# Later small transfers, a split first weight and identity matmuls in TensorE's pauses in a two-layer encoder trunk

## The chip, the cores and the metric

The kernel runs on one core of a Trainium2 chip. The metric is the device time of one execution in microseconds (us), the median over several runs. The profile is one further execution, recorded by the hardware profiler.

## What is computed

The reference runs two layers over 256 tokens of width 1024, in float32. Each layer is three sublayers, and each sublayer ends in a LayerNorm of the scaled residual plus the sublayer's output.

```python
for i in range(DEPTH):
    ...
    h = layer_norm(ALPHA * h + mix, ln_g[i, 0], ln_b[i, 0])
    h = layer_norm(ALPHA * h + memory_attention(h, mem, ...), ln_g[i, 1], ln_b[i, 1])
    if i % 2 == 0:
        ffn = swiglu(h, ffn_w_gate[j], ffn_w_up[j], ffn_w_down[j])
    else:
        ffn = moe_swiglu(h, moe_router[j], moe_w_gate[j], moe_w_up[j], moe_w_down[j])
    h = layer_norm(ALPHA * h + ffn, ln_g[i, 2], ln_b[i, 2])
```

Layer 0 mixes tokens with a sliding-window attention with sinks beside a stick-breaking attention, layer 1 with a forgetting attention. Layer 1 ends in a mixture of experts: a router (1024 to 8 columns) picks two of eight experts for each token, and each expert is a SwiGLU of width 3584.

## The kernel before

**Products.** All weights stream from device memory in chunks of 128 rows times up to four row tiles, 512 columns wide (1 MB; the first two chunks of all are half as large). SyncE issues the loads in order, with six buffers `raw`. A float32 product is made of three passes of a faster format: ScalarE copies a chunk to `w_hi` (line 1088), VectorE subtracts it from the original to get `w_lo` (lines 1456 and 1944), and TensorE multiplies high by high, high by low and low by high (lines 379 to 381). The semaphores `hi_made` and `lo_made` count the chunks that are split. The activations are split the same way: TensorE transposes 128x128 tiles of `X` into PSUM against the identity `ident` (line 423), ScalarE copies them to `xT_hi` (1088, called from `split_to`), VectorE makes `xT_lo` (1462). Four PSUM banks hold the eight tiles, two tiles each, so there are four copies of each kind, numbered 0 to 3 below. Chunk 0 of the first product needs copy 0 alone, chunk 1 copy 1, chunk 2 copies 2 and 3.

**Order.** The order of each engine's work is written out by hand, one function for each engine, and every engine runs its own list in that order. Waits are semaphores. A wait at the head of an engine's list holds back all that stands behind it on that engine, and nothing on the others.

**The start.** GpSimd writes the identity (lines 938 and 939), issues three small transfers (sinks of 4 KB, gate bias of 8 KB, `f_w` of 64 KB, lines 940 to 942) and builds masks, until it waits for `dist_abs` from VectorE (line 959). TensorE does 8 matmuls of the identity with itself (line 451; their output is overwritten), 16 transposes of `X` as its two halves land, 8 more identity matmuls (line 459), and then waits for the first chunk. ScalarE does the four `xT_hi` copies and then the splits; VectorE does two `xT_lo`, the first chunk's `w_lo`, and then the other two `xT_lo` (lines 1533 to 1536).

**The pauses.** At the end of the memory attention of each layer the function `normed_T` (lines 609 and 707) transposes the normalised `X`. The tokens are two blocks of 128, `t` = 0 and 1. VectorE normalises block 0 (`norm`, ending in line 1502), TensorE transposes its eight tiles, VectorE normalises block 1, and TensorE does the other eight. The other two LayerNorms of a layer put matmuls of the memory's key and value product around the transposes (`normed_T_beside`).

In layer 1 the router follows. `narrow` (lines 428 to 446) is a product of 24 small matmuls (lines 436 to 438), a copy of its result to `e_h` by VectorE (line 1440), and two small transposes (line 444). VectorE then finds the two experts of each token (lines 1814 to 1825), TensorE counts tokens by expert with five small matmuls (lines 746 to 753, "places"), VectorE makes the selection matrix `pick` (line 1835), and TensorE picks the first expert's rows with 16 matmuls in two halves (line 765, `pick_rows`). ScalarE and VectorE split the picked rows into `xe_hi` and `xe_lo`, half by half, and the experts' matmuls start.

Of the kernel before, what the change touches and what calls it, by code (L numbers as in the profile page):

```python
# [22 lines left out]
ALU = mybir.AluOpType  # L23
# [3 lines left out]
P = 128  # L27
# [4 lines left out]
def trunk(nc, x, mem, ln_g, ln_b, mem_wq, mem_wkv, mem_wo, ab_w_in, ab_sinks, ab_w_out,  # L32
# [76 lines left out]
    with ExitStack() as ctx:  # L109
# [144 lines left out]
        def sem(name):  # L254
            if name not in sems:
                sems[name] = ctx.enter_context(nc.semaphore(name))
            return sems[name]
# [101 lines left out]
        def _(pe):  # L359
# [52 lines left out]
            def transposes(key, src, tiles, b0, ready=None):  # L412


                dst = [claim(pe, f"{key}.{q // 2}", b0 + q // 2) for q in range(0, tiles, 2)]
                for t in range(TB):
                    for k in range(tiles):
                        if ready is not None and k % (tiles // 2) == 0:

                            name, n = ready[t]  # L420
                            pe.wait_ge(name, n if k else n - 1)
                        c = (k % 2) * SEQ + t * P
                        m = nc.tensor.transpose(dst[k // 2][:, c:c + P], src[:, t, k * P:(k + 1) * P],  # L423
                                                ident[:, :])
                        if t == TB - 1 and (k % 2 or k == tiles - 1):
                            m.then_inc(filled[b0 + k // 2], 1)

            def narrow(name, w_h, w_l, n, ready, staged, sb):
# [11 lines left out]
                m.then_inc(filled[4], 1)  # L440
                pe.wait_ge(sem(staged), 1)
# [5 lines left out]

            pe.wait_ge(sem("ident_made"), 1)

            for _ in range(8):  # L450
                nc.tensor.matmul(bank[7][:, 0:P], ident[:, :], ident[:, :], start=True, stop=True,
                                 skip_group_check=True)
# [5 lines left out]
            for _ in range(8):  # L458
                nc.tensor.matmul(bank[7][:, 0:P], ident[:, :], ident[:, :], start=True, stop=True,
                                 skip_group_check=True)  # L460
# [9 lines left out]
            for l in range(2):  # L470
# [138 lines left out]
                def normed_T(key, n):  # L609

                    transposes(key, X, KT, 4, ready=[(sem("normed"), NORMED * n + 2 * (t + 1)) for t in range(TB)])
# [95 lines left out]
                normed_T(f"{l}n1", 3 * l + 1)  # L707
# [34 lines left out]
            narrow("router", r_hi, r_lo, NE, ready, "r_T_made", e_h[0])  # L742
# [44 lines left out]

            pe.wait_ge(sem("picked"), 1)
# [134 lines left out]
        def _(pool):  # L923
# [8 lines left out]
            def link(ins):  # L932
# [7 lines left out]
            pool.dma_start(sinks[:, :], ab_sinks[0].partition_broadcast(P)).then_inc(sem("sink_in"), 16)  # L940
            pool.dma_start(gate_b[:, :], c_b_f[0].partition_broadcast(P)).then_inc(sem("b_in"), 16)
            pool.dma_start(f_w[:, :, :], c_w_in[0][:, 3 * D:3 * D + CH].rearrange("(k p) c -> p k c", p=P))\
                .then_inc(sem("f_in"), 16)
# [14 lines left out]

            pool.wait_ge(sem("dist_abs"), 1)
# [123 lines left out]
        def _(act):  # L1083
# [27 lines left out]
            def split_to(key, hi, tiles=range(4)):  # L1111

                for q in tiles:
                    b = wait_filled(act, f"{key}.{q}")
                    copy(hi[:, 2 * q:2 * q + 2, :].rearrange("p k t -> p (k t)"), b[:, :])\
                        .then_inc(sem("t_hi"), 1)
# [24 lines left out]
            split_to("0x", xT_hi)  # L1141
# [285 lines left out]
        def _(dve):  # L1427
# [114 lines left out]
            dve.wait_ge(sem("sink_in"), 16)  # L1542
            link(nc.vector.tensor_scalar(neg_sinks[:, :], sinks[:, :], -1.0, None, ALU.mult))

            for l in range(2):
# [59 lines left out]
                if l == 0:  # L1605
                    dve.wait_ge(sem("masks0"), 2)
                us = units(l)
# [427 lines left out]
```

## Time and profile before

| | |
|---|---|
| runs, us | 1654.07, 1654.28, 1656.89 |
| median, us | 1654.28 |
| the profiled execution, us | 1653.97 |
| its span from first to last instruction, us | 1652.0 |
| mean granted TensorE clock | 0.991 of full speed |
| TensorE matmul busy | 97% of the span |
| VectorE busy | 77% |
| ScalarE busy | 63% |
| GpSimd busy | 7% |

The page calls TensorE's matmuls PE and its weight loads PEld, VectorE DVE, ScalarE ACT, GpSimd POOL, SyncE SP. All positions in time are counted from the start of the span. The experts' part runs from about 678 us to the end; what comes before is the two layers' attention and layer 0's feed-forward part. The granted clock is given as a share of 2.4 GHz: 1.00 is 2.4 GHz and 0.50 is 1.2 GHz.

### The profile page before, as it was taken

Reading aid. Unit: us, or ns where it says so; the run is one execution under the profiler, and the core shown is the slowest. Engines: PE = TensorE matmul, PEld = TensorE weight load, DVE = VectorE, ACT = ScalarE, POOL = GpSimd, SP = SyncE. Lnnn points to the kernel's source line nnn. Section 1 sums busy time; section 2 is a strip of 40 time slices with the busy share of each in tenths; the row PEclk is TensorE's granted clock in tenths of the full one; section 3 lists DMA queues with packets and bytes.
Section 4 is the critical chain, followed back from the end, with each engine's and each line's share of the span. In section 5 each row is a group of like instructions: output and inputs, shape, how many; then the busy total and the mean of one; then the engine's idle time right before and its main releaser. Section 6 shows DMA issues by size and latency. Waiting matters only on the chain.

```text
span 1652.0 us, 21357 instructions
## 1 busy us (share of the span) xinstructions
PE 1605.9 (97%) x7602; PEld 1321.5 (80%) x7602; DVE 1269.3 (77%) x1188; ACT 1035.8 (63%) x935; POOL 118.3 (7%) x129
## 2 busy tenths in 40 slices
PE   8999999999999999999999999999999999999997
PEld 7777878888787687788888888888888888888775
DVE  5687565454746676789889889888888988988996
ACT  4464544443445543668777777777777777777673
POOL 2102010000113201000000000000000000000120
PEclk9999999999999999899999999999999999999999
DMA  9537655466455462899999999999999999999992
GB/s 334 177 103 234 225 171 186 130 224 208 154 193 177 143 221 72 290 373 362 389 378 376 388 366 386 389 362 388 389 359 383 388 369 385 388 358 390 361 362 99
DMA packets 238104, 480.11 MB, mean 291 GB/s; under 512 B 8224, under 2 KB 11328, under 8 KB 238048
## 3 DMA queue, kind: packets, MB, share of 16 engines
q1 hardware_dynamic: 229744, 454.06, 76.9%
q0 software_dynamic: 6288, 21.63, 4.1%
q10 hardware_dynamic: 2016, 3.67, 0.6%
q8 instruction: 35, 0.57, 0.2%
q14 instruction: 21, 0.17, 0.0%
HBM read 473.54 MB, written 11.03 MB: 293 GB/s over the span
## 4 chain that ended last, share of the span: by engine, by line
PE 84%; DVE 7%; issue 5%; DMA 3%; ACT 1%; POOL 1%; DVEq 0%; SPq 0%; POOLq 0%; ACTq 0%
PE bank L379 26%; PE bank L381 26%; PE bank L380 26%; DMA c_add<-gate_rows 2%; PE bank L845 1%; DVE w_lo L1944 1%; PE bank L423 1%; PE bank L666 1%; PE bank L644 1%; DVE w_lo L1456 1%; DVE X L1493 1%; DVE X L1502 1%; POOL c_add L926 1%; DMA raw<-in_ab_w_in_dram 0%; DVE stats L1482 0%
## 5 line engine op out<-in xcount | busy, mean ns | idle before, releaser
L1088 ACT ACTIVATE w_hi<-raw 128x2048 fp32r<-128x2048 f32 (+1 forms) x322 | 608.7, 1895 | 231.8 <-PE bank L381 222.5
L1944 DVE TENSOR_TENSOR w_lo<-raw,w_hi 128x2048 fp32r<-128x2048 f32 x221 | 503.1, 2290 | 81.8 <-ACT w_hi L1088 78.5
L1456 DVE TENSOR_TENSOR w_lo<-raw,w_hi 128x2048 fp32r<-128x2048 f32 (+1 forms) x96 | 211.2, 2205 | 135.3 <-ACT w_hi L1088 135.2
L379 PE MATMUL bank<-w_hi,xe_hi 128*128 128x512 f32 x736 | 293.0, 398 | 1.5 <-DVE w_lo L1944 1.5
L381 PE MATMUL bank<-w_hi,xe_lo 128*128 128x512 f32 x736 | 288.0, 391 | 0.0
L380 PE MATMUL bank<-w_lo,xe_hi 128*128 128x512 f32 x736 | 287.2, 390 | 0.0
L379 PE MATMUL bank<-w_hi,xT_hi 128*128 128x512 f32 (+1 forms) x560 | 218.1, 390 | 3.6 <-DVE w_lo L1456 3.4
L380 PE MATMUL bank<-w_lo,xT_hi 128*128 128x512 f32 (+1 forms) x560 | 214.1, 382 | 0.0
L381 PE MATMUL bank<-w_hi,xT_lo 128*128 128x512 f32 (+1 forms) x560 | 214.0, 382 | 0.0
L381 PEld LDWEIGHTS bank<-w_hi,xe_lo 128*128 128x128 f32 x736 | 138.4, 188 | 29.9
L379 PEld LDWEIGHTS bank<-w_hi,xe_hi 128*128 128x128 f32 x736 | 138.7, 188 | 29.1 <-DVE w_lo L1944 1.9
L380 PEld LDWEIGHTS bank<-w_lo,xe_hi 128*128 128x128 f32 x736 | 138.8, 189 | 27.4
L1944 DVE TENSOR_TENSOR w_lo_more<-raw,w_hi_more 128x2048 fp32r<-128x2048 f32 x63 | 144.2, 2289 | 18.4 <-ACT w_hi_more L1088 11.3
L1088 ACT ACTIVATE w_hi_more<-raw 128x2048 fp32r<-128x2048 f32 x64 | 122.8, 1919 | 28.1 <-PE bank L381 23.9
L379 PE MATMUL bank<-w_hi,eT_hi 128*128 128x512 f32 x320 | 125.8, 393 | 0.4 <-DVE w_lo L1944 0.4
L379 PEld LDWEIGHTS bank<-w_hi,xT_hi 128*128 128x128 f32 x560 | 105.9, 189 | 24.6 <-issue 5.0
L381 PE MATMUL bank<-w_hi,eT_lo 128*128 128x512 f32 x320 | 124.6, 389 | 0.0
L380 PE MATMUL bank<-w_lo,eT_hi 128*128 128x512 f32 x320 | 124.6, 389 | 0.0
L381 PEld LDWEIGHTS bank<-w_hi,xT_lo 128*128 128x128 f32 x560 | 106.0, 189 | 20.7
L380 PEld LDWEIGHTS bank<-w_lo,xT_hi 128*128 128x128 f32 x560 | 106.1, 189 | 19.4
L1944 DVE TENSOR_TENSOR w_lo<-raw_more,w_hi 128x2048 fp32r<-128x2048 f32 x40 | 91.4, 2286 | 3.7 <-ACT w_hi L1088 3.7
L1088 ACT ACTIVATE w_hi<-raw_more 128x2048 fp32r<-128x2048 f32 x40 | 76.6, 1916 | 25.2 <-PE bank L381 25.2
(281 smaller groups left out, 2150.8 us busy)
## 6 DMA issues: line engine op xcount, KB each, us to landing
raw<-in_moe_w_gate_dram SPq DMA_DIRECT2D x96, 1024.0 KB, 9.0
raw<-in_moe_w_up_dram SPq DMA_DIRECT2D x96, 1024.0 KB, 8.3
raw<-in_moe_w_down_dram SPq DMA_DIRECT2D x96, 1024.0 KB, 7.0
raw<-in_mem_wkv_dram SPq DMA_DIRECT2D x16, 1024.0 KB, 5.0
raw_more<-in_moe_w_up_dram SPq DMA_DIRECT2D x16, 1024.0 KB, 8.6
raw_more<-in_moe_w_gate_dram SPq DMA_DIRECT2D x16, 1024.0 KB, 8.6
raw_more<-in_moe_w_down_dram SPq DMA_DIRECT2D x16, 1024.0 KB, 7.4
raw<-in_c_w_in_dram SPq DMA_DIRECT2D x12, 1024.0 KB, 5.0
```

Of the source, the lines that this page charges most:

```text
L379: nc.tensor.matmul(d, xh, hi[:, k, :], start=(first and k == 0), stop=False)
L380: nc.tensor.matmul(d, xh, lo[:, k, :], start=False, stop=False)
L381: m = nc.tensor.matmul(d, xl, hi[:, k, :], start=False, stop=(last and k == n - 1))
L423: m = nc.tensor.transpose(dst[k // 2][:, c:c + P], src[:, t, k * P:(k + 1) * P], ident[:, :])
L644: m = nc.tensor.matmul(d[:, t * SEQ:(t + 1) * SEQ], QK[:, 2 * h + k, t * P:(t + 1) * P], MK[:, 2 * h + k, :], start=(k == 0), stop=(k == 1))
L666: m = nc.tensor.matmul(d[:, k * SEQ:(k + 1) * SEQ], MV[:, mb, c:c + P], PT_t[i % 2][:, mb * SEQ:(mb + 1) * SEQ], start=(mb == 0), stop=(mb ...
L845: m = nc.tensor.transpose(d[:, q * P:(q + 1) * P], e_h[j % 2][:, q * P:(q + 1) * P], ident[:, :])
L926: return nc.gpsimd.affine_select(out=dst, in_=dst, pattern=[[step, width]], compare_op=op, fill=fill, base=base, channel_multiplier=cm)
L1088: return nc.scalar.activation(dst, src, ACT.Copy)
L1456: tt(w_lo[s][:, 0:n], raw[c % NRAW][:, 0:n], w_hi[s][:, 0:n].bitcast(F32), ALU.subtract).then_inc(lo_made, 1)
L1493: link(nc.vector.scalar_tensor_tensor(out=xt, in0=xt, scalar=mean_var[:, t, 0:1], in1=gb[:, 0, :], op0=ALU.subtract, op1=ALU.mult))
L1944: tt(w_lo[s][:, :], raw_exp[r][:, :], w_hi[s][:, :].bitcast(F32), ALU.subtract).then_inc(lo_made, 1)
```

## The change

The three small transfers of GpSimd move behind its first masks, and behind a wait for the first three weight chunks to be split. VectorE's use of the sinks moves behind the layer 0 projections. ScalarE makes `w_hi` of the first chunk between copies 1 and 2 of `xT_hi`. The identity matmuls become a function, `keep_busy(bank, n)`, which issues `n` of them: at the start 16 and not 8 stand before the first product; 32 stand between the two blocks' transposes in `normed_T` of both layers' `n1`; and in the router 6 stand after its product, 14 after its transposes, and 8 after the places.

```diff
-            def transposes(key, src, tiles, b0, ready=None):
+            def transposes(key, src, tiles, b0, ready=None, busy=None):
                 dst = [claim(pe, f"{key}.{q // 2}", b0 + q // 2) for q in range(0, tiles, 2)]
                 for t in range(TB):
+                    if t and busy is not None:
+                        busy()
                     for k in range(tiles):
...
                 m.then_inc(filled[4], 1)
+                if busy is not None:
+                    keep_busy(busy, 6)
                 pe.wait_ge(sem(staged), 1)
...
+            def keep_busy(b, n):
+
+                for _ in range(n):
+                    nc.tensor.matmul(bank[b][:, 0:P], ident[:, :], ident[:, :], start=True, stop=True,
+                                     skip_group_check=True)
+
             pe.wait_ge(sem("ident_made"), 1)
-            for _ in range(8):
-                nc.tensor.matmul(bank[7][:, 0:P], ident[:, :], ident[:, :], start=True, stop=True,
-                                 skip_group_check=True)
+            keep_busy(7, 8)
...
-            for _ in range(8):
-                nc.tensor.matmul(bank[7][:, 0:P], ident[:, :], ident[:, :], start=True, stop=True,
-                                 skip_group_check=True)
+            keep_busy(7, 16)
...
-                normed_T(f"{l}n1", 3 * l + 1)
+                def mw0_bank(l=l):
+
+                    wait_emptied(pe, f"{l}mw0.0")
+                    return fillings[f"{l}mw0.0"][0]
+
+                normed_T(f"{l}n1", 3 * l + 1, busy=lambda: keep_busy(mw0_bank(), 32))
...
-            narrow("router", r_hi, r_lo, NE, ready, "r_T_made", e_h[0])
+            free = fillings["1mw0.0"][0]
+            narrow("router", r_hi, r_lo, NE, ready, "r_T_made", e_h[0], busy=free)
+            keep_busy(free, 14)
             pe.wait_ge(sem("taken_made"), 1)
...
+            keep_busy(free, 8)
             pe.wait_ge(sem("picked"), 1)
             pick_rows("xA")
...
-            pool.dma_start(sinks[:, :], ab_sinks[0].partition_broadcast(P)).then_inc(sem("sink_in"), 16)
-            pool.dma_start(gate_b[:, :], c_b_f[0].partition_broadcast(P)).then_inc(sem("b_in"), 16)
-            pool.dma_start(f_w[:, :, :], c_w_in[0][:, 3 * D:3 * D + CH].rearrange("(k p) c -> p k c", p=P))\
-                .then_inc(sem("f_in"), 16)
...
             nc.gpsimd.nop().then_inc(sem("masks0"), 1)
 
+            pool.wait_ge(lo_made, NSPL)
+            pool.dma_start(sinks[:, :], ab_sinks[0].partition_broadcast(P)).then_inc(sem("sink_in"), 16)
+            pool.dma_start(gate_b[:, :], c_b_f[0].partition_broadcast(P)).then_inc(sem("b_in"), 16)
+            pool.dma_start(f_w[:, :, :], c_w_in[0][:, 3 * D:3 * D + CH].rearrange("(k p) c -> p k c", p=P))\
+                .then_inc(sem("f_in"), 16)
             pool.wait_ge(sem("dist_abs"), 1)
...
-            split_to("0x", xT_hi)
+            split_to("0x", xT_hi, (0, 1))
+            split(0)
+            split_to("0x", xT_hi, (2, 3))
             split(NSPL - 1)
...
-            dve.wait_ge(sem("sink_in"), 16)
-            link(nc.vector.tensor_scalar(neg_sinks[:, :], sinks[:, :], -1.0, None, ALU.mult))
...
                 if l == 0:
                     dve.wait_ge(sem("masks0"), 2)
+                    dve.wait_ge(sem("sink_in"), 16)
+                    link(nc.vector.tensor_scalar(neg_sinks[:, :], sinks[:, :], -1.0, None, ALU.mult))
```

What stands on TensorE around `normed_T` of layer 0, before:

```order
L381 MATMUL bank<-w_hi_57,xT_lo 128x512
L423 MATMUL bank<-ident,X 128x128 x16
L379 MATMUL bank<-w_hi_55,xT_hi 128x512
L380 MATMUL bank<-w_lo_58,xT_hi 128x512
L381 MATMUL bank<-w_hi_55,xT_lo 128x512
```

and after the change:

```order
L425 MATMUL bank<-ident,X 128x128 x8
L455 MATMUL bank<-ident 128x128 x32
L425 MATMUL bank<-ident,X 128x128 x8
L379 MATMUL bank<-w_hi_55,xT_hi 128x512
L380 MATMUL bank<-w_lo_58,xT_hi 128x512
```

The 16 transposes are parted by 32 identity matmuls, and the feed-forward product stands directly behind. On TensorE from the end of the router's product to the first expert's rows, before:

```order
L438 MATMUL bank<-xT_lo,r_hi 8x256
L444 MATMUL bank<-ident,e_h_133 128x8 x2
L746 MATMUL bank<-taken,tri_lt 128x8
L748 MATMUL bank<-taken,ones 128x8
L750 MATMUL bank<-taken,tri_lt 128x8
L753 MATMUL bank<-taken,ones 128x8 x2
L765 MATMUL bank<-pick,X 128x128 x16
```

and after the change, with other line numbers for the same work:

```order
L440 MATMUL bank<-xT_lo,r_hi 8x256
L455 MATMUL bank<-ident 128x128 x6
L448 MATMUL bank<-ident,e_h_133 128x8 x2
L455 MATMUL bank<-ident 128x128 x14
L760 MATMUL bank<-taken,tri_lt 128x8
L762 MATMUL bank<-taken,ones 128x8
L764 MATMUL bank<-taken,tri_lt 128x8
L767 MATMUL bank<-taken,ones 128x8 x2
L455 MATMUL bank<-ident 128x128 x8
L779 MATMUL bank<-pick,X 128x128 x16
```

Three groups of identity matmuls now stand ahead of the transposes, the places and the picked rows. Nothing else moves on TensorE but the larger group at the start.

## Rows read from the trace of the kernel before

**Rows 1.** The page, its first part: busy time, share of the span, instructions.

```profile
PE 1605.9 (97%) x7602; PEld 1321.5 (80%) x7602; DVE 1269.3 (77%) x1188; ACT 1035.8 (63%) x935; POOL 118.3 (7%) x129
```

**Rows 2.** TensorE's waits: line, what it waited for, us in total, times, longest.

```profile
PE bank L423 <- DVE X L1502: 8.1, 3, 3.9
```

**Rows 3.** Timeline, first 13 us: start, duration, instructions, idle time before and releaser.

```profile
3.84 0.59 SPq L874 DMA_DIRECT2D mem_tok<-in_mem_dram  x1
...
6.70 2.06 ACT L1088 ACTIVATE xT_hi<-bank 128x512 fp32r<-128x512 f32 x4 [4.60 <-PE bank L423]
...
7.59 1.95 PE L459 MATMUL bank<-ident 128*128 128x128 f32 x16
9.94 1.06 ACT L1088 ACTIVATE w_hi<-raw 128x1024 fp32r<-128x1024 f32 x1 [1.17 <-DMA raw<-in_ab_w_in_dram]
11.02 1.23 DVE L1456 TENSOR_TENSOR w_lo<-raw,w_hi 128x1024 fp32r<-128x1024 f32 x1 [2.40 <-ACT w_hi L1088]
...
12.51 0.47 PE L379 MATMUL bank<-w_hi,xT_hi 128*128 128x512 f32 x1 [2.97 <-DVE w_lo L1456]
```

**Rows 4.** Groups of instructions, 7.5 to 9.6 us: busy us, mean ns of one, idle.

```profile
L459 PE MATMUL bank<-ident 128*128 128x128 f32 x16 | 1.9, 275 | 0.0
```

**Rows 5.** DMA queues from 6 to 10 us: packets, MB, share of 16 engines' time.

```profile
q0 software_dynamic: 83, 0.06, 24.0%
```

**Rows 6.** One stretch: busy time of each engine, then granted clock, DMA share, GB/s.

```profile
13.50:16.50 3.00, 3.00 (x8) 2.32 (x8) 1.08 (x1) 1.91 (x1) 0.00 (x0) 0.50 1.03 382
```

**Rows 7.** Timeline: TensorE's transposes of the memory, and its next wait.

```profile
19.70 1.91 PE L423 MATMUL bank<-ident,mem_tok 128*128 128x128 f32 x16
...
27.52 0.36 PE L379 MATMUL bank<-w_hi,xT_hi 128*128 128x256 f32 x1 [0.42 <-DVE w_lo L1456]
```

**Rows 8.** DMA issues, first 12 us: the memory tokens, size, us from issue to landing.

```profile
mem_tok<-in_mem_dram SPq DMA_DIRECT2D x1, 1024.0 KB, 13.3
```

**Rows 9.** Timeline of TensorE around `normed_T` of layer 0.

```profile
226.15 1.03 PE L423 MATMUL bank<-ident,X 128*128 128x128 f32 x8
231.11 1.78 PE L423 MATMUL bank<-ident,X 128*128 128x128 f32 x8 [3.93 <-DVE X L1502]
233.05 0.77 PE L379 MATMUL bank<-w_hi,xT_hi 128*128 128x512 f32 x1 [0.17 <-DVE xT_lo L1462]
```

**Rows 10.** The chain of waits there: start, duration, what.

```profile
233.82 0.43 PE bank L380
...
235.45 0.23 PE bank L381
```

**Rows 11.** Timeline in layer 1, from `normed_T` to the experts.

```profile
660.03 1.97 PE L423 MATMUL bank<-ident,X 128*128 128x128 f32 x8 [3.93 <-DVE X L1502]
...
661.38 2.48 DVE L1462 TENSOR_TENSOR xT_lo<-bank,xT_hi 128x512 fp32r<-128x512 f32 x4 [0.75 <-ACT xT_hi L1088]
...
662.22 0.37 PE L436 MATMUL bank<-xT_hi,r_hi 128*8 128x256 f32 x1 [0.23 <-DVE xT_lo L1462]
...
667.26 0.29 PE L444 MATMUL bank<-ident,e_h 8*128 8x8 f32 x2 [0.72 <-DVEq L1525]
...
669.32 0.59 PE L746 MATMUL bank<-taken,tri_lt 128*128 128x8 f32 x2 [1.77 <-DVE taken L1823]
...
672.49 5.28 PE L765 MATMUL bank<-pick,X 128*128 128x128 f32 x32 [0.87 <-DVE pick L1835]
...
676.02 0.60 ACT L1088 ACTIVATE xe_hi<-bank 128x512 fp32r<-128x512 f32 x1 [6.44 <-PE bank L765]
...
677.65 0.49 PE L379 MATMUL bank<-w_hi,xe_hi 128*128 128x512 f32 x1
```

**Rows 12.** Stretches of the same place, columns as in rows 6.

```profile
660.00:664.00 4.00, 3.74 (x17) 2.70 (x18) 3.12 (x5) 3.25 (x5) 1.58 (x3) 0.50 0.40 143
...
670.00:674.00 4.00, 3.13 (x15) 3.04 (x16) 2.04 (x9) 0.00 (x0) 0.00 (x0) 0.50 0.99 374
```

**Rows 13.** Same columns, in the last expert.

```profile
1544.00:1546.00 2.00, 2.00 (x6) 1.51 (x6) 2.00 (x1) 0.00 (x0) 0.00 (x0) 0.52 0.51 122
```

More of the change, by code:

```diff
@@ L426, in transposes, with narrow @@
                             m.then_inc(filled[b0 + k // 2], 1)
-            def narrow(name, w_h, w_l, n, ready, staged, sb):
+            def narrow(name, w_h, w_l, n, ready, staged, sb, busy=None):
                 dst = claim(pe, f"{name}0", 4)
@@ L607, in _, with normed_T @@
                 pair[0] = kv_pair + (1 if l == 0 else 2)
-                def normed_T(key, n):
-                    transposes(key, X, KT, 4, ready=[(sem("normed"), NORMED * n + 2 * (t + 1)) for t in range(TB)])
+                def normed_T(key, n, busy=None):
+                    transposes(key, X, KT, 4, ready=[(sem("normed"), NORMED * n + 2 * (t + 1)) for t in range(TB)],
+                               busy=busy)
                 def normed_T_beside(key, n, name):
```

## The prediction

> **What bounds the kernel now.** I read the page's busy shares first. TensorE is busy in 97% of the span [rows 1], so a change tells only where it starts TensorE's work earlier or later, lengthens it, or changes its clock. Then its waits [rows 2]: the longest group is on VectorE's normalisation, 8.1 us in three waits, up to 3.9 us each. The timelines show where. At the start TensorE ends its identity matmuls at 9.54 and starts the first product at 12.51, behind ScalarE's `w_hi`, which began at 9.94 as soon as the chunk had landed, and VectorE's `w_lo` [rows 3]. In each layer's `normed_T` it stands still for 3.93 us [rows 9, 11]. Behind the second follow pauses of 0.72, 1.77 and 0.87 us [rows 11]. After each pause the granted clock is at 0.50, that is 1.2 GHz, for a while: 13.50 to 16.50 [rows 6], from about 231.8 to 235.3 (matmul steps of 0.43, then 0.23 us) [rows 10], and in 660 to 664 and 670 to 674 [rows 12]. So the change is about four stalls and the slow stretches behind them.
>
> **The price of an identity matmul.** Eight of them are 16 records of 275 ns each, which overlap: together 1.95 us at full clock [rows 3, 4]. The spacing is (1.95 - 0.275) / 15 = 0.112 us a record, 0.223 us a matmul. At half clock the eight transposes of layer 1 give (1.97 - 0.47) / 7 = 0.21 a record (0.47 is an estimate of a slow record's own length, from slow steps of 0.43 [rows 10]), 0.43 a matmul. So at full clock 32 take 7.1 us, 16 take 3.6, 14 take 3.1, 8 take 1.8 and 6 take 1.3. TensorE's list is in order: what exceeds a pause delays what stands behind.
>
> **The start.** GpSimd's queue took 24.0% of the 16 DMA engines between 6 and 10 us, that is 0.96 us [rows 5]. Without it in front, the first chunk lands between 0.96 us earlier and no earlier; a row nearer than this there isn't, and I take 0.9: 9.0. `xT_hi` copies 0 and 1 end at 6.70 + 2.06 / 2 = 7.7 [rows 3], so ScalarE is free, and would be with all four (8.8). Its new order costs nothing: copies 2 and 3 end by 11.2, VectorE wants them behind `w_lo`, and TensorE only in chunk 2. `w_hi` runs 9.0 to 10.1, `w_lo` 10.2 to 11.4, and the first product starts at 11.6, 0.9 earlier. The 16 identity matmuls end at 7.59 + 3.6 = 11.2, just before: they cost nothing, but bar a gain above 1.3. With TensorE busy up to 0.4 us before, I take the clock to stay at 1.00. Before, the 24 matmuls of chunks 0 and 1 took 19.70 - 12.51 = 7.2 us [rows 3, 7]; at steps of 0.23 they take 5.5. That is 1.7 more. The memory's transposes then start at 17.1; their data were issued at 3.84 [rows 3] and landed 13.3 us later [rows 8], at 17.1, and land about 0.9 earlier now, so they don't wait. The next wait, 0.42 us at 27.52 [rows 7], hangs on these transposes by `mT_hi`, `w_hi` and `w_lo`, moves with them and stays. The later small transfers take the same 0.96 us of the DMA engines at about 18 to 28. There they meet chunks that TensorE needs 5.5 us apart, and the first chunks they meet are not waited for. GpSimd, which now stands at its new wait until about 17.5, has behind it in its list the masks that wait for VectorE until about 22 in any case; its three issues fit in between. VectorE's step on the sinks moves behind the projections, some 40 us later than the transfer lands. All this is nothing; without that slack it would be at most the 0.96 us again. **Start: -2.6 us**, between -1.7 (no earlier landing, clock kept) and -3.0.
>
> **Layer 0's pause.** The first eight transposes end at 231.11 - 3.93 = 227.18, their issue at 227.05. 32 identity matmuls last to 227.05 + 7.1 = 234.2, and only then come the other eight, at 231.11 before: 3.1 late [rows 9]. `X` is long ready, and the path from them to the product (1.94 us before) is about 0.1 shorter at full clock: the product starts at 236.0, 3.0 late. What the clock gives back is the slow stretch from 233.05 to 235.45: a first step of 0.77 and four of 0.35 to 0.43 in place of 0.47 and 0.23 [rows 3, 9, 10], together 1.0. All of TensorE's work behind follows without a pause, so nothing hides the rest. **Layer 0: +2.0 us**, between -1.1 (the pause exactly filled) and +3.0 (no clock gained).
>
> **Layer 1's pauses.** Step by step at full clock [rows 11]. The second transposes start 3.1 late, at 663.1. The router's product started 2.19 after them and did so on the first `xT_lo`; 0.1 shorter, it starts at 665.1. Its 24 matmuls at 0.113 take 2.7 (4.3 before; VectorE's four `xT_lo` need 2.48, and are not the limit), end 667.8 against 666.54: 1.3 late. Then 6 identity matmuls last 1.3, while the copy to `e_h` needed 0.72: the two transposes start at 669.1, 1.9 late. VectorE's search needed 2.06 from there to the places; 14 identity matmuls behind 0.2 us of transposes last 3.1: the places start at 672.4, 3.1 late. Their ten records take 1.2 and not 2.3 (669.32 to 672.49 less the 0.87 of idle time; the clock was at 0.50 [rows 12]): `pick` is ready 2.0 late, at 674.5. But 8 identity matmuls after the places (673.5) last to 675.3, so picking starts 2.8 late. Its 32 records take 3.6 and not 5.28: it ends at 678.9, as does the split of the first half (half the records 1.8, then the 1.63 us from 676.02 to 677.65). The experts start at 678.9 against 677.7. SyncE's load of the experts' seventh chunk waits for the router's product and is 1.3 late, like its use: nothing. **Layer 1: +1.2 us.** Between -4.4 (every pause exactly filled: product 1.7, places 1.0, picking 1.7 faster) and +12 (the clock lost, below).
>
> **The sum** is -2.6 + 2.0 + 1.2 = +0.6 us. The profiled execution's own time is 1653.97 with a span of 1652.0; 0.6 more is 1654.6. It is 0.3 below the median of the runs, so against the median it would be 1654.9; I take 1654.6. All other work keeps its place: the experts' part is a chain of matmuls that starts 0.6 later.
>
> **Rivals.** (1) **The fillers fit.** If an identity matmul took half of what I read, all five groups would end inside their pauses: -2.6 - 1.1 - 4.4 = -8.1 us, 1645.9. The Trainium skill ("TensorE: Matmul & The Clock Gate", Back-to-back issue gap) gives about 56 ns between 128-column matmuls at the full clock; by it the 64 records of 32 matmuls would take 3.6 us, less than the pause of 3.93. Against it stand the 16 records of rows 3 and 4 in this kernel, with the same operands, at twice that spacing. 8%. (2) **Slower: the clock falls in the router all the same.** Between the last transposes (664.0) and the router's product (665.1) a gap of 1 us stays. Before, 0.29 us of work between pauses of 0.72 and 1.77 was too little to keep the clock [rows 11, 12]. If it falls once in there, the identity matmuls at 0.43 last 2.6, 6.0 and 3.4 us, over 1.3, 3.1 and 1.8: 5.8 more, and the 1.6, 1.1 and 1.7 that I booked for a faster product, places and picking are gone too. Layer 1 is then +1.2 + 5.8 + 4.4 = +11.4, the whole +10.8: 1664.8. It decides from the clock at 665 on. 9%. (3) **A smaller start.** The chunk lands no earlier since other bytes take the room: -1.7, the sum +1.5, 1655.5. 15%, within 0.2%. (4) **More gained than booked,** by a first chunk that lands earlier than 9.0, overruns partly taken up by VectorE's waits, or the slow stretch in the last expert [rows 13], which cost about 1.7 us while TensorE was busy and need not come again: 1650 to 1652. 14%, half of it beyond 0.2%. (5) Both overruns a little longer, with a new wait for a chunk behind them since ScalarE's and VectorE's splits begin 3 us later: 1658. 6%, half of it beyond.
>
> **How the numbers follow.** My forecast, 1652.5 to 1656.5, has 48%. 0.2% is 3.3 us, about what a measurement here can tell from no change: 1651.0 to 1657.6 is "same". Faster: 8 + 7 = 15%. Slower: 9 + 3 = 12%. Same: 48 + 15 + 7 + 3 = 73%. The range of 8 in 10 reaches from case 4 to case 5: 1650.0 to 1658.0; cases 1 and 2 are outside.
>
> **What would show it.** The record of 32 identity matmuls should be 64 long and 7.1 us, in both layers, with transposes directly behind and no idle time there. The first product should start near 11.6 with the clock at 1.00 to 17. The small transfers should be issued near 17.5. The router's product should start near 663.1 + 2.0 less the 0.6 gained up to there (2.6 - 2.0), and the clock be 1.00 from 655 to 680. It would be wrong if identity matmuls ran at another spacing in a stretch of 64, or if the clock fell with TensorE busy.

## The result and the profile after

The changed kernel took 1657.82 us (median of 12 runs, 1654.79 to 1659.58). The kernel before, run beside it, took 1653.82 us (12 runs, 1650.48 to 1656.89). The ratio is 1.0021, with a 95% interval of 1.0014 to 1.0029: about 3.5 us slower (4.0 between the two medians), just above the 0.2% that I had set as the bound of "same". The profiled execution of the changed kernel took 1659.53 us with a span of 1657.6 and a granted clock of 0.994. That is 5.6 us more than the span of before, 1652.0.

The first line of the page, against [rows 1]:

```profile
PE 1623.4 (98%) x7802; PEld 1340.4 (81%) x7802; DVE 1269.2 (77%) x1188; ACT 1036.2 (63%) x935; POOL 120.2 (7%) x129
```

There are 200 more matmul records, and TensorE is busy for 17.5 us more. The group of stalls of [rows 2] has gone, and the kernel is none the faster for it. The timeline of the first 17 us, against [rows 3, 7]:

```profile
7.42 3.74 PE L455 MATMUL bank<-ident 128*128 128x128 f32 x32
7.80 1.06 ACT L1104 ACTIVATE w_hi<-raw 128x1024 fp32r<-128x1024 f32 x1 [0.37 <-DMA raw<-in_ab_w_in_dram]
...
8.89 1.22 DVE L1474 TENSOR_TENSOR w_lo<-raw,w_hi 128x1024 fp32r<-128x1024 f32 x1 [0.62 <-ACT w_hi L1104]
...
10.91 0.48 PE L379 MATMUL bank<-w_hi,xT_hi 128*128 128x512 f32 x1
...
16.41 0.72 POOL L971 DMA_DIRECT2D sinks<-in_ab_sinks_dram  x1 [11.48 <-DVE w_lo L1474]
16.47 1.91 PE L425 MATMUL bank<-ident,mem_tok 128*128 128x128 f32 x16
```

`w_hi` begins 2.14 us earlier and the first product 1.60 us earlier. `w_lo` ends at 10.11, but TensorE is at its identity matmuls until about 10.9. The memory's transposes come 3.23 us earlier. What the small transfers took from the weight stream shows in the DMA queues from 6 to 10 us (packets, MB, share of the 16 engines' time), before and after:

```profile
q1 hardware_dynamic: 484, 0.94, 69.6%
q0 software_dynamic: 83, 0.06, 24.0%
```

```profile
q1 hardware_dynamic: 812, 1.60, 104.5%
```

Queue q1 is the weight stream, q0 is GpSimd's (the profile's shares can come out a little above 100%). With 0.06 MB of q0 beside it, the stream moved 0.66 MB less.

The timeline in layer 0, against [rows 9]:

```profile
224.18 1.03 PE L425 MATMUL bank<-ident,X 128*128 128x128 f32 x8
...
225.05 7.31 PE L455 MATMUL bank<-ident 128*128 128x128 f32 x64
...
228.33 1.41 DVE L1520 SCALAR_TENSOR_TENSOR X<-X,rstd,gb 128x512 f32<-128x512 f32 x2
...
232.20 1.04 PE L425 MATMUL bank<-ident,X 128*128 128x128 f32 x8
...
234.08 0.47 PE L379 MATMUL bank<-w_hi,xT_hi 128*128 128x512 f32 x1 [0.85 <-DVE xT_lo L1480]
```

VectorE has `X` ready at 229.74, and TensorE takes it up at 232.20. In between it works at nothing that anyone needs. The same place in layer 1, up to the experts, against [rows 11]:

```profile
659.04 1.03 PE L425 MATMUL bank<-ident,X 128*128 128x128 f32 x8
...
659.91 7.31 PE L455 MATMUL bank<-ident 128*128 128x128 f32 x64
...
667.06 1.04 PE L425 MATMUL bank<-ident,X 128*128 128x128 f32 x8
...
668.94 0.28 PE L438 MATMUL bank<-xT_hi,r_hi 128*8 128x256 f32 x1 [0.85 <-DVE xT_lo L1480]
...
671.68 1.50 PE L455 MATMUL bank<-ident 128*128 128x128 f32 x12
...
673.11 0.29 PE L448 MATMUL bank<-ident,e_h 8*128 8x8 f32 x2
...
673.33 3.39 PE L455 MATMUL bank<-ident 128*128 128x128 f32 x28
...
676.56 0.29 PE L760 MATMUL bank<-taken,tri_lt 128*128 128x8 f32 x2
...
679.46 3.74 PE L779 MATMUL bank<-pick,X 128*128 128x128 f32 x32
683.17 0.49 PE L379 MATMUL bank<-w_hi,xe_hi 128*128 128x512 f32 x1
```

The clock, against [rows 12]: stretches of after (length, PE, PEld, DVE, ACT and POOL busy, then the granted clock, DMA share and GB/s). The last row lies in layer 1's `normed_T`, the first three in the two mixers, where the profile of before has 1.00:

```profile
78.00:80.00 2.00, 2.00 (x11) 1.34 (x8) 1.44 (x9) 2.00 (x4) 0.00 (x0) 0.50 0.03 11
428.00:430.00 2.00, 1.10 (x3) 0.92 (x4) 2.00 (x4) 2.00 (x3) 0.00 (x0) 0.76 0.04 7
556.00:558.00 2.00, 1.37 (x8) 0.86 (x8) 2.00 (x3) 1.40 (x6) 0.00 (x0) 0.50 0.00 0
662.00:664.00 2.00, 2.00 (x20) 2.00 (x20) 1.86 (x6) 0.00 (x0) 0.00 (x0) 1.00 0.03 8
```

So the clock held where identity matmuls stand, and fell at three places where the diff changes nothing.

**Where the time is.** I cut every profile at the same six instructions of TensorE: one behind the first scores of layer 0's mixer (near 78), a weight wait near 159, the transposes of layer 0's `n2` (near 426), a weight wait near 588, the `e_h` wait of the last expert (near 1528) and a `y` wait near 1638. Each number is the distance in us from one cut to the next; the kernels are described below.

```
kernel             to 78   78-159  159-426  426-588  588-1528  1528-1638
                                   (pause             (router)
                                    layer 0)
before             78.59   80.82   266.61   162.25   939.61    110.57
before again  e5   76.82   81.79   267.47   163.98   938.14    110.17
after              75.28   82.15   268.60   166.26   941.13    110.62
after again   e1   76.06   80.78   268.60   163.06   941.12    110.22
start only    e2   75.35   80.84   266.48   162.27   939.43    110.10
pauses only   e3   77.69   80.75   268.57   164.57   941.25    110.65
layer 0 only  e6   78.58   80.76   268.59   162.64   940.23    110.21
layer 1 only  e7   77.89   82.16   267.47   163.90   941.03    111.12
transfers     e8   75.09   82.06   267.30   163.90   938.37    110.17
fit           e4   75.60   80.84   265.65   164.25   935.80    110.40
fit, no router e12 75.95   80.76   265.63   163.02   938.31    110.65
```

The stretches that the diff doesn't touch go with the granted clock. From 78 to 159 us the profiles with a fall near 80 (e5, after, e7, e8) take 81.79 to 82.16, and those without 80.75 to 80.84. From 426 to 588 before and e2 have no fall and take 162.25 and 162.27; e1, e6 and e12, with some 3.4 us at half clock, take 162.64 to 163.06; e5, e7, e8 and e4, with about 7 us, take 163.90 to 164.25; after, with some 10 us in two places, takes 166.26. Only e3 is long (164.57) without a fall.

In the profile the changed places sum to -3.3 (start) + 2.0 (layer 0) + 1.5 (layer 1) = +0.2 us. The other +5.4 lie in 78 to 159 (+1.3) and 426 to 588 (+4.0), in code that the diff doesn't touch. The experiments ask whether the change brings these on.

### The profile page after: what moved, and what is told of

Its sections match the earlier page's. It is cut to its first block, busy times and chain, and to the rows that moved or that the text cites. A ratio compares the mean times of both kernels' runs of the same rounds, so it can differ in the third digit from the quotient of the medians.

```text
span 1657.6 us, 21757 instructions
## 1 busy us (share of the span) xinstructions
PE 1623.4 (98%) x7802; PEld 1340.4 (81%) x7802; DVE 1269.2 (77%) x1188; ACT 1036.2 (63%) x935; POOL 120.2 (7%) x129
## 3 DMA queue, kind: packets, MB, share of 16 engines
HBM read 473.54 MB, written 11.03 MB: 292 GB/s over the span
## 4 chain that ended last, share of the span: by engine, by line
PE 84%; DVE 6%; issue 5%; DMA 2%; ACT 1%; POOL 1%; DVEq 0%; ACTq 0%; POOLq 0%
PE bank L379 25%; PE bank L381 25%; PE bank L380 25%; DVE w_lo L1962 2%; PE bank L455 2%; DMA c_add<-gate_rows 2%; PE bank L860 1%; PE bank L425 1%; PE bank L673 1%; PE bank L651 1%; DVE w_lo L1474 1%; POOL c_add L941 1%; DMA y_got<-y_rows,row_i 0%; DVE X L1511 0%; PE bank L545 0%
## 5 line engine op out<-in xcount | busy, mean ns | idle before, releaser
L1104 ACT ACTIVATE w_hi_more<-raw 128x2048 fp32r<-128x2048 f32 x64 | 122.9, 1920 | 28.0 <-PE bank L381 23.8
```

The source lines that it names most:

```text
L1104: return nc.scalar.activation(dst, src, ACT.Copy)
```

## The experiments

The runs of one chip share the runs of the kernel before: e1 to e4 (before 1654.6), e5 to e8 (1654.3), e9 to e12 (1654.17). Each median is of 11 or 12 executions, but of 5 in e3 and e4. "By the ratio" means the measured ratio times the time of before; it differs from the distance of the medians by up to 0.9 us.

### e1: the changed kernel again

No edit.

> The changed kernel once more, for a second profile and more times beside the others. In its first profile the granted clock fell to 0.50 at about 78, 429.5 and 556 us, in the attention parts, which the change does not touch; the kernel before had no such stretch there and one at 1543. Theory A (the places of these stretches differ from run to run and are chance): in this profile they lie elsewhere or are fewer, the offset to the kernel before is -3.3 us from the start, +2.0 from layer 0's pause and +1.5 from layer 1's, and the median lies 0 to 2 us above the kernel before. Theory B (the change brings them on, since TensorE comes to the attention parts without a slow stretch before): they come again at the same places, and the median lies 3 to 5 us above.

Measured: 1656.58 us (11 runs), ratio 1.0011 (1.0002 to 1.0020), 2.0 us over before; span of the profile 1653.4. The stretches 78 to 159 and 426 to 588 are back at 80.78 and 163.06, near those of before, while the two pauses stand where they stood (268.60 and 941.12). The start takes 76.06, 0.8 more than in the first profile. So most of the +5.4 belonged to that execution, and not to the kernel.

### e2: the start alone

```diff
-                normed_T(f"{l}n1", 3 * l + 1, busy=lambda: keep_busy(mw0_bank(), 32))
+                normed_T(f"{l}n1", 3 * l + 1)
...
-            narrow("router", r_hi, r_lo, NE, ready, "r_T_made", e_h[0], busy=free)
-            keep_busy(free, 14)
+            narrow("router", r_hi, r_lo, NE, ready, "r_T_made", e_h[0])
...
-            keep_busy(free, 8)
```

> The kernel before with the start's part of the change alone: later small transfers, ScalarE's new order, 16 identity matmuls. My theory: the first product at 10.9 us as in the changed kernel, the offset to the kernel before -3.3 us until layer 0's pause, and all of it kept: median 1650.5, 3.3 us faster. Rival (slow stretches in the attention parts come with the early start): the clock falls near 78 us in the profile and the median gains only 1 to 2 us.

Measured: 1652.17 us, ratio 0.9990 (0.9981 to 0.9999); span 1648.0, 4.0 under that of before, of which the start has 3.24. In the medians 2.4 us are gained (1.7 by the ratio), less than my 3.3, though the clock does not fall near 78 us as the rival had it.

### e3: the pauses alone

The start is that of before (small transfers early, ScalarE's old order, 8 identity matmuls); the 32, 6, 14 and 8 stay.

```diff
-            keep_busy(7, 16)
+            keep_busy(7, 8)
...
-            split_to("0x", xT_hi, (0, 1))
-            split(0)
-            split_to("0x", xT_hi, (2, 3))
+            split_to("0x", xT_hi)
```

> The kernel before with the identity matmuls in the pauses alone (32, 32, 6, 14, 8), the start as before. My theory: +2.0 us in layer 0 and +1.5 in layer 1, median 3.5 us above the kernel before. Rival (the fillers also bring on slow stretches in layer 1's attention): 5 to 7 us above, with the clock at 0.50 near 430 or 555 us.

Measured: 1659.95 us, ratio 1.0035 (1.0021 to 1.0049), 5.3 us slower: the rival's 5 to 7, but without its falls of the clock. In place the two pauses cost 1.96 and 1.64 against the profile of before. Another 2.3 lie in 426 to 588, where the clock of this execution did not fall. GpSimd waited longer there for its transfers of the gates. Its waits from 520 to 556 us (what it waited for, then total, times, longest), before and then e3:

```profile
POOL c_add L926 <- DMA c_add<-gate_rows: 14.8, 6, 3.2
```

```profile
POOL c_add L941 <- DMA c_add<-gate_rows: 17.1, 6, 4.1
```

This is 2.3 us more for six transfers of the same size, in the same place. The changed kernel's profile has 17.0 there. From its first mask on `c_add` behind 513 us to its last before 555, GpSimd took 37.4 us in before, 39.7 in e3 and 38.9 in after. In the whole stretch TensorE waited 2.2 us for VectorE's `P` in e3 and 0.6 in before. That the late gates cause these waits is likely, since VectorE adds `c_add` to the scores that `P` is made from; no run alters the gates alone.

### e4: the same groups, sized to the pauses

At 0.223 us each, 17 take 3.8 us, 3 take 0.7, 7 take 1.6 and 4 take 0.9.

```diff
-                    keep_busy(busy, 6)
+                    keep_busy(busy, 3)
...
-                normed_T(f"{l}n1", 3 * l + 1, busy=lambda: keep_busy(mw0_bank(), 32))
+                normed_T(f"{l}n1", 3 * l + 1, busy=lambda: keep_busy(mw0_bank(), 17))
...
-            keep_busy(free, 14)
+            keep_busy(free, 7)
...
-            keep_busy(free, 8)
+            keep_busy(free, 4)
```

> The changed kernel with the groups in the pauses cut to what the pauses hold: 17, 17, 3, 7 and 4 identity matmuls at 0.223 us. My theory (the loss in the pauses is the overrun, and shorter groups keep the clock as well): layer 0's pause costs -1.1 us instead of +2.0, layer 1's -4 instead of +1.5; median 8 us below the changed kernel and 5 to 8 below the kernel before. Rival (the shorter groups leave enough idle time for the clock to fall): the clock is at 0.50 behind a pause and the gain over the kernel before is 3 us or less.

Measured: **1647.62 us** (1646.45 to 1648.23, 5 runs), ratio 0.9954 (0.9941 to 0.9968), 7.0 us faster than before. This version beats both kernels. Its timeline, layer 0 and then the router:

```profile
228.17 1.32 PE L425 MATMUL bank<-ident,X 128*128 128x128 f32 x8
...
230.11 0.47 PE L379 MATMUL bank<-w_hi,xT_hi 128*128 128x512 f32 x1 [0.62 <-DVE xT_lo L1480]
...
660.06 0.28 PE L438 MATMUL bank<-xT_hi,r_hi 128*8 128x256 f32 x1 [0.62 <-DVE xT_lo L1480]
...
662.80 0.83 PE L455 MATMUL bank<-ident 128*128 128x128 f32 x6
...
663.68 0.29 PE L448 MATMUL bank<-ident,e_h 8*128 8x8 f32 x2
...
663.90 1.83 PE L455 MATMUL bank<-ident 128*128 128x128 f32 x14
...
665.74 0.39 PE L760 MATMUL bank<-taken,tri_lt 128*128 128x8 f32 x2
...
667.89 3.84 PE L779 MATMUL bank<-pick,X 128*128 128x128 f32 x32
```

The 32 picking records take 3.84 us, and not the 5.28 of [rows 11]. Layer 0's stretch is 0.96 under that of before, the router's 3.81 under; against the means below over the profiles without groups it is 1.4 and 3.4. The mechanism of the change is sound; its numbers are about twice too large.

### e5: the kernel before again

No edit. The question was whether the falls in the mixers come without the change.

> The kernel before once more, for a second profile of it. Open after the first five profiles: layer 1's mixer, from the wait near 426 to the one near 588 us, took 162.25 and 162.27 us in the two kernels without identity matmuls in the pauses and 163.1, 164.3, 164.6 and 166.3 us in the four with them. Theory A (chance: it is clock falls and GpSimd's waits for its gate transfers, which come in some executions of any kernel): this profile has 162 to 166 too, and as likely over 163 as not. Theory B (the groups bring it on): 162.3 again.

Measured: 1653.91 us, ratio 0.9998 (0.9988 to 1.0009). Its stretches of 80 to 82 and 556 to 558, columns as above:

```profile
80.00:82.00 2.00, 2.00 (x5) 1.61 (x6) 1.93 (x11) 1.65 (x2) 0.73 (x1) 0.50 0.00 0
556.00:558.00 2.00, 2.00 (x11) 2.00 (x10) 1.74 (x7) 0.12 (x1) 0.00 (x0) 0.50 0.46 108
```

The kernel before has both falls itself in this execution, with 81.79 and 163.98 in the two stretches. The theory that the change brings them on has fallen.

### e6 and e7: the pauses of one layer alone

Both have the start of before. e6 fills layer 0's pause only:

```diff
-                normed_T(f"{l}n1", 3 * l + 1, busy=lambda: keep_busy(mw0_bank(), 32))
+                normed_T(f"{l}n1", 3 * l + 1, busy=(lambda: keep_busy(mw0_bank(), 32)) if l == 0 else None)
```

> The kernel before with the 32 identity matmuls in layer 0's pause alone. My theory: from the wait near 159 to the one near 426 us 268.6 us instead of 266.6, so +2.0, and the rest as in the kernel before: median 1.5 to 2.5 us above it. Theory B of the run before (the group brings on a longer mixer in layer 1): 163 to 166 us from 426 to 588 and a median 3.5 to 5 above.

e7 fills those of layer 1 (`if l == 1`, and the 6, 14 and 8).

> The kernel before with the identity matmuls in layer 1's pause and in the router alone (32, 6, 14, 8). My theory: from the wait near 588 us to the one in the last expert near 1528 941.1 us instead of 939.6, so +1.5, median 1 to 2 us above the kernel before. Layer 1's mixer stands before these groups in TensorE's list, so by theory B it takes 162.3 us; by theory A anything from 162 to 166.

Measured: e6 1658.55 us, ratio 1.0022 (1.0010 to 1.0033); e7 1657.51, ratio 1.0014 (1.0005 to 1.0023). By ratio that is 3.6 and 2.3 us over before, and both are above what I expected. In place e6 has +2.0 in its pause and e7 +1.4 in its own, as predicted. The profile of e6 has a span 2.5 over that of before, so the median's other microsecond or more isn't in the execution that was profiled.

The table shows one more thing. With the groups of the change a stretch is always the same (268.57 to 268.62, and 941.00 to 941.25, with e9 below). Without any it varies: 266.48 to 267.47 (five profiles, mean 267.07) and 938.14 to 940.23 (five, mean 939.16), since the clock behind a pause is down for longer in one execution than in the next. Around layer 0's pause it is below 1.00 from 230 to 236 us in the first profile of before, with 0.95, 0.50 and 0.69 in its three stretches of 2 us, and from 228 to 236 in e5, with 0.77, 0.50, 0.50 and 0.53. Against the means the groups cost 1.5 and 2.0 us.

The start varies in the same way. To the first cut, the five profiles with the old start (before, e5, e3, e6, e7) take 76.82 to 78.59, mean 77.91; the five with the whole new one (after, e1, e2, e4, e12) take 75.28 to 76.06, mean 75.65. That is -2.3 and not -3.3.

### e8: only the small transfers moved

Of the change, only GpSimd's three transfers, and VectorE's use of the sinks, are moved. 8 identity matmuls and ScalarE's order are as before.

> The kernel before with the later small transfers alone (ScalarE's order and 8 identity matmuls as before). If the early landing is what the start gains by, the first chunk's w_hi can begin only at about 8.5 us, behind all four xT_hi copies, instead of 7.8; the first product starts near 11.6 and TensorE stands idle from about 9.4 to then. My theory: the clock still falls behind that idle time as in the kernel before, so the start gains 0.9 to 1.3 us instead of 3.3. Rival (2.2 us of idle time are too few for a fall): 2.6 us.

Measured: 1651.50 us, ratio 0.9982 (0.9974 to 0.9991), 3.0 us faster by the ratio and 2.8 by the medians. That is the rival's gain and not mine. Its first product:

```profile
8.16 1.06 ACT L1102 ACTIVATE w_hi<-raw 128x1024 fp32r<-128x1024 f32 x1
...
10.74 0.47 PE L379 MATMUL bank<-w_hi,xT_hi 128*128 128x512 f32 x1 [1.76 <-DVE w_lo L1470]
```

```profile
11.00:13.00 2.00, 2.00 (x10) 1.62 (x10) 1.80 (x3) 0.85 (x1) 0.00 (x0) 1.00 1.03 421
```

The first product is 0.17 us earlier than in the profile of the whole change. The clock holds behind an idle time of 1.76 us, where it fell behind 2.97 [rows 3, 6] (it fell behind 2.57 in e3, and held behind 2.49 in e5). So all that the start gains here comes from the transfers. ScalarE's order and the 8 more identity matmuls bring nothing here. The 16 even hold the product back: in all five profiles of the whole new start it stands directly behind them, 0.55 to 1.16 us after `w_lo` ended (0.80 in after, 0.94 in e1, 1.16 in e12), where it follows 0.26 us behind in e8. They begin only when the transposes of `X` are done, at 7.42 in after and at 8.19 in e1. This run is faster than e2 in the medians too, by 0.7 us on another chip, which is less than I would call shown.

### e9: the changed kernel with the mixers' pauses covered

Groups of 5, 3, 2, 9 and 6 identity matmuls stand in addition where the clock fell, near 78, 555 and 428 us.

```diff
                     d = claim(pe, f"{l}t{i}", b)
+                    keep_busy(b, {(0, 1): 5, (1, 13): 3, (1, 14): 2}.get((l, i), 0))
+                    pe.wait_ge(sem(f"p_ready{l}"), i + 1)
...
+                    if (l, p) == (1, 6):
+                        keep_busy(7, 9)
...
+                    if key == "0n2":
+                        wait_emptied(pe, "0dn1.0")
+                        keep_busy(fillings["0dn1.0"][0], 6)
```

> The changed kernel with more identity matmuls, sized to the waits, where the profiles show chance falls of the clock: 5 in layer 0's mixer (before the second head's transposes, a wait of 1.27 us), 6 behind layer 0's last normalisation (1.55 us), and 3, 9 and 2 at the end of layer 1's mixer (0.74, 2.28, 0.61 us). What the runs so far leave open: by its parts in the profiles (-3.3 start, +1.5 to +2.0 layer 0, +1.5 to +2.0 layer 1) the changed kernel should be level with the kernel before, its median is 2 to 4 us above. Theory (chance falls in the mixers make up the rest and the spread): no fall at 78, 430 and 555 us in the profile, median 2 to 3 us below the changed kernel's 1656.6 to 1657.8, so 1654 to 1655, spread under 2 us. Rival (the rest is elsewhere): median above 1656.

Measured: 1656.22 us, ratio 1.0013 (1.0004 to 1.0022). The three falls are gone from its profile, and the kernel is still 2 us over before, as the rival had it. The profile shows the clock down in the last expert, near 1544, where before and e1 have it too, and near 1588, where neither does:

```profile
1544.00:1546.00 2.00, 2.00 (x6) 1.52 (x6) 2.00 (x2) 0.00 (x0) 0.00 (x0) 0.50 0.68 255
1588.00:1590.00 2.00, 2.00 (x7) 1.54 (x6) 2.00 (x3) 0.00 (x0) 1.89 (x1) 0.50 0.92 224
```

Its last stretch (1528 to 1638) is 112.24 against 110.57 of before. I had expected 1654 to 1655; the rest over before isn't in those three falls.

### e10 and e11: the sized groups with the mixers covered

e10 is e4 with the additions of e9. e11 has 12 at the start in place of 16.

> The kernel with groups cut to the pauses (17, 17, 3, 7, 4) with the same additions in the mixers. Theory: 1 to 3 us below the 1647.6 of the cut groups alone, so 1645 to 1647, with falls only in the last expert and at the end. Rival: no lower than 1647.6.

> The same with 12 identity matmuls in front of the first product in place of 16. In the changed kernel the first product started at 10.91 us, 0.8 behind the first w_lo, held by the 16; with later transfers alone and 8 it started at 10.74. Theory: the first product at 10.3, 0.5 us earlier than with 16, median 0.3 to 0.6 lower. Rival: with less cover the clock falls behind the start, 1 us slower.

Measured: e10 1649.69 us, ratio 0.9974 (0.9963 to 0.9984); e11 1649.10, ratio 0.9970 (0.9961 to 0.9980). Both gain some 4 to 5 us over before, and neither is better than e4 (7.0, on another chip). In e10's profile the clock falls near 126, and near 1580 behind a wait for VectorE that is 1.45 us long in before:

```profile
1579.53 0.80 PE L379 MATMUL bank<-w_hi,xe_hi 128*128 128x512 f32 x1 [3.49 <-DVE w_lo L1968]
```

Covering the mixers is not worth its lines. Whether 12 at the start would do better than 16 stays open: the first chunk happened to be split later in e11's profile, whose first product is at 11.03 behind an idle time of 0.97.

### e12: the sized groups without the router's

```diff
-            narrow("router", r_hi, r_lo, NE, ready, "r_T_made", e_h[0], busy=free)
-            keep_busy(free, 7)
+            narrow("router", r_hi, r_lo, NE, ready, "r_T_made", e_h[0])
...
-            keep_busy(free, 4)
```

> The changed kernel with 17 identity matmuls in each normed_T and none in the router. It tells what the router's groups bring once they fit. Theory (the clock falls behind the router's pauses of 0.7 and 1.8 us whether or not the one before is covered): a slow stretch near 670 us, the router's part 938 us or more from the wait near 588 to the one near 1525 in place of 935.8, median 2 to 3 us above the cut groups' 1647.6. Rival (17 in normed_T are enough to carry the clock over the router's pauses): level with it.

Measured: 1649.76 us, ratio 0.9973 (0.9964 to 0.9982). The clock is down in the router's picking again:

```profile
666.89 6.79 PE L778 MATMUL bank<-pick,X 128*128 128x128 f32 x32 [0.87 <-DVE pick L1851]
```

```profile
668.00:670.00 2.00, 2.00 (x11) 2.00 (x11) 1.73 (x1) 0.00 (x0) 0.00 (x0) 0.50 1.05 408
```

The router's stretch is 938.31 against e4's 935.80. The 3, 7 and 4 together bring 2.5 us there, and 2.1 in the medians. The medians are less certain: e4 ran on another chip with 5 executions, and e10, which has the router's groups and the covered mixers and ran beside e12, is level with it.

## Why the prediction was right, and where it was not

The measured time lies inside the range (1650.0 to 1658.0), near its upper end. The forecast of +0.6 us was too low: by the ratio it measured +3.5, and +1.8 in the second comparison. By my own bound of 0.2% the first is just "slower" and the second "same". That the time lies inside the range is in part luck. The upper end stood for rival (5), longer overruns and a new wait for a chunk. The overruns were as forecast, and layer 0's stretch, with +1.99 for +2.0, leaves no room for such a wait; what took the time up there was something else, told below.

**The price of an identity matmul was right.** 64 records take 7.31 us in both layers, for 7.1 predicted; the spacing of 0.112 us read from 16 records holds for 64. Rival (1), that the groups fit, was wrong for the changed kernel. e4 shows what such a fit gives: 1647.6, where I had put 1645.9. Against the profile of before layer 0 then gains 0.96 (for 1.1) and layer 1 gains 3.8 (for 4.4). By the means it is 1.4, 3.4 and 2.3 at the start, 7.1 in all, where the medians show 7.0. Of the two prices that the prediction weighed, the 56 ns that the Trainium skill ("TensorE: Matmul & The Clock Gate", Back-to-back issue gap) gives for an isolated matmul of 128 columns and the 112 ns of the row, the row was the one to follow. The same section gives about 81 ns for a stream in which each matmul has its weight load, as here; by that the 64 records would take 5.2 us, an estimate, and not fit the pause either.

**Layer 0 was right:** +2.0 predicted, +1.99 in the profile. Counted from the first transposes, the second begin 8.02 us later, against 4.96 before: 3.06 late. The product behind them is 3.0 late (9.90 against 6.90), and 1.0 comes back by the clock.

**Layer 1 was right within 0.3 us,** at each step. Counted from the first transposes (655.07 before, 659.04 after), the places start at 17.5 (predicted 17.3), the picking at 20.4 (20.2) and the experts at 24.1 (23.8; before 22.6). Each is late by what the group in front exceeds its pause. Of the losses here, the last group's is the plainest: `pick` is ready at 678.55, and TensorE starts on it at 679.46.

**Rival (2) did not come about.** The clock stays at 1.00 through the router. It did not fall behind the 0.85 us of idle time that remain before its product (668.94). Nor did rival (3): the first chunk landed earlier. Of rival (4) the early landing came about and the time did not.

**The start was mis-sized against the profile:** -3.3, for -2.6 predicted and -3.0 as the end of its range. The term that failed is the landing of the first chunk. I had priced the small transfers by their share of the DMA engines, 0.96 us, and put the landing at 9.0. It was at 7.80, 2.1 us earlier than before. One execution overstates it, though. With the old start `w_hi` began between 9.07 and 9.94 in five profiles, mean 9.60, and with the whole new one between 7.80 and 8.43, mean 8.15: 1.5 us earlier, for the 0.9 in my sum. The engines' share understates what such transfers cost the stream beside them: from 6 to 10 us the stream moved 0.87 to 1.01 MB in those five and 1.44 to 1.61 MB in the other five and e8. The second term is the clock's part. It was 1.7 predicted and measured 1.63 (the memory's transposes 5.56 us behind the first product, for 7.19), but in e5 the clock of the kernel before doesn't fall at the start, behind 2.49 us of idle time, and there was nothing to give back. By the means of five profiles the start is worth 2.3. The later small transfers and ScalarE's order, priced at nothing, cost nothing that a profile shows. I was right that the 16 identity matmuls could bar a gain above 1.3 (they held it at 1.6), but gave them no price. The third term is theirs: they hold the product back by 0.3 to 0.9 us, and the clock keeps without the 8 more in e8.

**The last expert's slow stretch costs nothing.** In rival (4) I put 1.7 us on it [rows 13]. The stretch from 1528 to 1638 takes 110.10 to 110.57 with it (before, e1, e2, e5, e6, e8, e4) and no less without it (110.62 in after, 110.65 in e3, 111.12 in e7). VectorE's `w_lo` is the later one there: TensorE's wait for it near 1585 is 1.45 us in before and 1.13 in e1, and 2.06 in after and 2.10 in e3, where no slow stretch precedes it.

**The sum failed in what it left out.** I wrote that all other work keeps its place. In the profiled executions the changed stretches sum to +0.2. But the code between them takes a different time from execution to execution, by 1.4 us (80.75 to 82.16) from 78 to 159 and by 4.0 us (162.25 to 166.26) from 426 to 588; the two profiles of the kernel before are 1.0 and 1.7 apart there. One profile against another can therefore mislead by more than the effect in question. This explains the profile's +5.6: falls of the clock near 80, 430 and 556 us and probably, by some 1.5 us, GpSimd's slower gates. The clock carries the spread of the times too. Of the executions of before beside e5 to e8, the 12 with a mean granted clock of 0.989 or less took 1655.4 us on average, and the 7 with 0.992 or more 1652.0. It doesn't fully explain the medians. By the means, the pauses cost +3.5 (1.5 and 2.0) and the start brings -2.3, which gives +1.2, where +1.8 to +3.5 is measured. The parts, by the ratio +3.6 (e6), +2.3 (e7) and -3.0 (e8) or -1.7 (e2), make +2.9 to +4.2, which agrees with the whole, but e6 and e7 are each more than their stretches show (1.5 and 2.0). What carries this remainder **stays open**. Candidates are GpSimd's waits for its gate transfers in layer 1's mixer (17.0 against 14.8 us) and VectorE's chain in the last expert. e9 rules out that the three falls of the clock in the mixers are all of it.

## What to carry to other kernels

Identity matmuls that keep the clock up pay when they end inside the pause, so count the records that the profile shows (two for each float32 matmul here), take their spacing, and size each group: fitted, the kernel gained 7.0 us (some 2.3 of them at the start, by the small transfers), and with about twice the number it lost 2 to 3.5. Move small transfers out from in front of the load that the first work waits for, even if their share of the DMA engines looks like nothing. Where an effect is a few microseconds, compare stretches of several profiles, cut at the same instructions, before a difference is put down to the change.

## What the runs showed of the hardware that I had not expected

- The same kernel has a fall of the granted clock in one execution and none in the next: near 81 and 556 us in e5, and not in the first profile of the same kernel; at the start in the first profile, behind 2.97 us of idle time, and in e3, e7 and e6, behind 2.57, 2.93 and 3.12, but not in e5, behind 2.49.
- The length of the last pause does not settle it alone. Behind 1.76 and 2.49 us idle at the start the clock stayed at 1.00 (e8, e5); behind 0.72 and 1.77 us with 0.29 us of work between it fell [rows 11, 12], and it fell near 556 us, where TensorE's longest wait from 553 to 560 was under 2.4 us.
- With the falls in the mixers covered, others came that before does not have: near 126 and 1580 in e10, near 1588 in e9. That the cover brings them on is not shown; e12, without it, has one near 1580 too.
- GpSimd's three small transfers, 0.06 MB, delayed the first 0.5 MB chunk by 1.5 us (means of five profiles with the old start and five with the new), though they took 0.96 us of the DMA engines in the first profile.
